# Adding rows on GpSimd ahead of the products with ones, in the second block of a two-block layer

## The reference

```python
def second_block(x, w_in, ...):
    h = rms_norm(x, pre_mix_g)
    a, gate, q, k, v = split(h @ w_in)
    yc = conformer_conv_group(a, gate, ...)       # 1024 channels
    ya = neighbourhood_attention_group(q, k, v, rpb)
    mix = concatenate([yc, ya]) @ w_out
    x = x + rms_norm(mix, post_mix_g)             # the MLP's rows
    h = rms_norm(x, pre_mlp_g)
    f = square(relu(h @ w_up)) @ w_down
    return x + rms_norm(f, post_mlp_g)

def conformer_conv_group(a, gate, ...):
    u = depthwise_conv(a * sigmoid(gate), 31 taps) + b_dw
    return silu(layer_norm(u, ln_g, ln_b))        # over the 1024 channels
```

## Time and profile before

| | us |
|---|---|
| timed runs | 2861.81, 2864.57, 2866.37 |
| median | 2864.57 |
| span of the profiled execution | 2856.0 |
| TensorE busy in it | 2747.0 (96%) |
| VectorE busy in it | 2033.0 (71%) |
| ScalarE busy in it | 1360.4 (48%) |
| GpSimd busy in it | 208.1 (7%) |

### The profile page before, as it was taken

One profiled execution on the slowest core, in us unless ns is written; L12 is line 12 of the kernel. 1 busy time (PEld: TensorE's weight loads), 2 busy tenths in 40 slices (PEclk: granted clock), 3 DMA queues, 4 the chain that ended last, 5 costly groups with the idle time before them and its releaser, 6 DMA issues.

```text
span 2856.0 us, 43985 instructions
## 1 busy us (share of the span) xinstructions
PE 2747.0 (96%) x17404; PEld 2439.8 (85%) x17404; DVE 2033.0 (71%) x2983; ACT 1360.4 (48%) x2169; POOL 208.1 (7%) x180
## 2 busy tenths in 40 slices
PE   6988999999999999999999999999999999999997
PEld 6888778888889888888888889998788888888886
DVE  7898786777797886555556688996567566575665
ACT  3445653343444544444444554465654444444454
POOL 0231000000002000000000080111110000000001
PEclk9999999999999999999999999999999999999999
DMA  9864255656787686555555555554445555555553
GB/s 392 314 228 134 95 172 186 198 192 206 236 304 268 217 305 226 191 188 188 191 185 192 187 169 169 177 165 139 153 130 182 190 187 191 187 190 189 188 190 127
DMA packets 158461, 565.31 MB, mean 198 GB/s; under 512 B 17584, under 2 KB 21936, under 8 KB 158256
## 3 DMA queue, kind: packets, MB, share of 16 engines
q1 hardware_dynamic: 158256, 562.50, 58.9%
HBM read 560.33 MB, written 2.10 MB: 197 GB/s over the span
## 4 chain that ended last, share of the span: by engine, by line
PE 85%; DVE 9%; ACT 3%; issue 2%; DMA 1%; SPq 0%; POOL 0%; DVEq 0%; ACTq 0%; POOLq 0%
PE BK L350 20%; PE BK L348 19%; PE BK L351 10%; PE BK L347 10%; PE BK L353 6%; PE BK L355 5%; PE BK L354 5%; DVE LO L657 2%; PE BK L435 2%; ACT HI L517 1%; DVE ADA L653 1%; DVE B L865 1%; DVE B L707 1%; PE BK L360 1%; PE BK L461 1%
## 5 line engine op out<-in xcount | busy, mean ns | idle before, releaser
L517 ACT ACTIVATE HI<-RAW 128x1024 fp32r<-128x1024 f32 x825 | 875.1, 1061 | 1253.7 <-PE BK L348 862.3
L657 DVE TENSOR_TENSOR LO<-RAW,HI 128x1024 fp32r<-128x1024 f32 x825 | 1017.9, 1234 | 376.2 <-ACT HI L517 373.0
L350 PE MATMUL BK<-H,HI 128*128 128x512 f32 x2528 | 1009.5, 401 | 9.0 <-DVE LO L657 8.5
L348 PE MATMUL BK<-H,HI 128*128 128x512 f32 x2496 | 985.3, 396 | 0.0
L351 PE MATMUL BK<-H,LO 128*128 128x256 f32 x2528 | 703.0, 278 | 0.0
L347 PE MATMUL BK<-H,LO 128*128 128x256 f32 x2496 | 698.2, 280 | 0.4 <-DVE H L703 0.2
L353 PE MATMUL BK<-H,HI 128*128 128x256 f32 x1840 | 545.6, 296 | 33.6 <-DVE B L707 15.7
L347 PEld LDWEIGHTS BK<-H,LO 128*128 128x128 f32 x2496 | 469.7, 188 | 111.8 <-DVE H L703 2.0
L351 PEld LDWEIGHTS BK<-H,LO 128*128 128x128 f32 x2528 | 477.0, 189 | 99.7 <-issue 1.0
L354 PE MATMUL BK<-H,HI 128*128 128x256 f32 x1840 | 523.8, 285 | 0.0
L355 PE MATMUL BK<-H,LO 128*128 128x256 f32 x1840 | 523.6, 285 | 0.0
(11 more groups left out here) (244 smaller groups left out, 1870.5 us busy)
## 6 DMA issues: line engine op xcount, KB each, us to landing
RAW<-wst_dram SPq DMA_DIRECT2D x825, 512.0 KB, 3.9
RAW<-wada_dram SPq DMA_DIRECT2D x155, 512.0 KB, 4.5
EARLY<-wada_dram SPq DMA_DIRECT2D x37, 512.0 KB, 7.8
EARLY<-wst_dram SPq DMA_DIRECT2D x33, 512.0 KB, 6.7
X<-xT_dram SPq DMA_DIRECT2D x8, 512.0 KB, 8.8
B<-bias_dram SPq DMA_DIRECT2D x32, 128.0 KB, 3.4
out_dram<-X SPq DMA_DIRECT2D x3, 512.0 KB, 2.7
CN<-consts_dram SPq DMA_DIRECT2D x1, 840.0 KB, 8.1
```

Of the source, the lines that this page charges most:

```text
L348: e.matmul(bk[:, :], hh, H[:, k, :], start=False, stop=last, skip_group_check=True).then_inc(S["tile"], 1)
L350: e.matmul(bk[:, :], hh, H[:, k, :], start=first, stop=False, skip_group_check=True)
L517: e.activation(HI[:, u % NHL, :], raw_at(slot), ACT.Copy).then_inc(S["hi"], 1)
L657: e.tensor_tensor(LO[:, u % NHL, :], raw_at(slot), HI[:, u % NHL, :].bitcast(f32), sub).then_inc(S["lo"], 1)
```

## The change

GpSimd gets two new steps. `conv_add` adds two rows of 128x256, with its own semaphore `cv_g`. `rows_add` adds a pair of rows (128x512) into another pair. With them:

- The convolution's rows are added into CSUM, row to row, as each pair's taps end, seven additions in all; `conv_sum` is then one product.
- The first centred square goes to CSQ without a buffer of TE, the other seven squares are added to it, and one product (`conv_sum` again) takes the place of eight. It is emitted behind the last addition, at the place where the eighth product stood. A buffer of TE is free again when its addition is done.
- In `mlp_rows` the squares of pairs 2 to 7 and the last are added into rows 0 and 1, seven additions of 128x512, and two products at the end take the place of sixteen.

```diff
--- before.py
+++ after.py
@@ -193,7 +193,7 @@
 
 SIGNALS = ("tile", "hi", "lo", "ada", "mod_p", "mod_v", "pre_a", "pre_v", "ev_a", "ev_v", "ev_g", "ev_p",
            "st_a", "st_v", "st_g", "st_p", "ad_v", "l2_a", "l2_v", "l2_p", "gd_p", "gd_a", "gd_v", "at_p", "at_a",
-           "at_v", "at_g", "cv_a", "cv_v", "cv_p", "spin")
+           "at_v", "at_g", "cv_a", "cv_v", "cv_p", "cv_g", "spin")
 LOADS = tuple(f"raw{i}" for i in range(NRAW + NEARLY)) + tuple(f"bias{i}" for i in range(4)) + ("cols", "consts", "x", "pos", "x2", "out")
 
 
@@ -283,6 +283,7 @@
         CA = [B1[:, 9 + j, :] for j in range(8)]
         BB = [B2[:, 13 + i, :] for i in range(4)]
         MEAN = B2[:, 17, :]
+        CSUM, CSQ = B1[:, 17, :], B1[:, 18, :]
         Y = [B2[:, i, :] for i in range(16)]
         Z = [B1[:, i, :] for i in (8, 9, 10, 11, 16, 17, 18, 19)]
         YA = [B2[:, i, :] for i in range(16)]
@@ -489,21 +490,15 @@
                     r = e.matmul(bk[o:o + 64, 128 * qb:128 * qb + 128], vt[:, c, o:o + 64], t[:, 128 * c:128 * c + 128], start=(c == 0), stop=(c == 1))
                 r.then_inc(S["at_p"], 1)
 
-            def conv_sum(bk, ready, free):
+            def conv_sum(bk, src, ready, free):
                 q.wait_ge(ready, free)
-                for j in range(8):
-                    r = e.matmul(bk[:, 0:256], cn("ones"), CA[j], start=(j == 0), stop=(j == 7))
-                r.then_inc(S["cv_p"], 1)
-
-            def conv_square_sum(bk, j, t, square, free):
-                q.wait_ge(square, free)
-                e.matmul(bk[:, 0:256], cn("ones"), t, start=(j == 0), stop=(j == 7)).then_inc(S["cv_p"], 1)
+                e.matmul(bk[:, 0:256], cn("ones"), src, start=True, stop=True).then_inc(S["cv_p"], 1)
 
             walk(dict(tile=tile, mod_sum=mod_sum, spin=spin, stat_add=stat_add, stat_sum=stat_sum, acc2_sum=acc2_sum, rope_turn=rope_turn, ba_turn=ba_turn,
                       cumulate=cumulate, row_sum=row_sum, spread=spread, g_spread=g_spread, g_heads=g_heads, g_turn=g_turn,
                       g_turn_mt=g_turn_mt, g_pair=g_pair, g_ws=g_ws, g_state=g_state, g_out=g_out, turn=turn,
                       mla_scores=mla_scores, mla_values=mla_values, norm_turn=norm_turn, na_scores=na_scores, na_values=na_values,
-                      conv_sum=conv_sum, conv_square_sum=conv_square_sum))
+                      conv_sum=conv_sum))
 
         def scalar(e):
             q = Engine(e, S)
@@ -914,11 +909,19 @@
                 q.wait_ge(loaded)
                 e.tensor_tensor(BB[i % 4], BB[i % 4], cn("nm"), add).then_inc(S["at_g"], 1)
 
+            def conv_add(dst, a, b, ready, free, before):
+                q.wait_ge(ready, free, before)
+                e.tensor_tensor(dst, a, b, add).then_inc(S["cv_g"], 1)
+
+            def rows_add(dst, src, squares, before):
+                q.wait_ge(squares, before)
+                e.tensor_tensor(dst, dst, src, add).then_inc(S["st_g"], 1)
+
             def part_add(dst, t, copied):
                 q.wait_ge(copied)
                 e.tensor_tensor(dst, dst, t, add).then_inc(S["ev_g"], 1)
 
-            walk(dict(part_add=part_add, square_add=square_add, scaled_square=scaled_square, bias_mask=bias_mask))
+            walk(dict(part_add=part_add, conv_add=conv_add, rows_add=rows_add, square_add=square_add, scaled_square=scaled_square, bias_mask=bias_mask))
 
         def walk(mine, log=None):
             w = Walk(mine)
@@ -2015,25 +2018,36 @@
                         if n % CONV_STEP == 0:
                             yield
                     conv_tok[a:a + 2] = k
+                    if a == 0:
+                        csum = do("conv_add", "cv_g", CSUM, CA[0], CA[1], k, b2_free, None)
+                    else:
+                        csum = do("conv_add", "cv_g", CSUM, CSUM, CA[a], k, None, csum)
+                        csum = do("conv_add", "cv_g", CSUM, CSUM, CA[a + 1], k, None, csum)
                 for _ in xg:
                     yield
-                later(conv_norm(conv_tok[7]), 2)
+                later(conv_norm(csum), 2)
 
             def conv_norm(ready):
                 bi, bk, fr = mbank.get()
-                m = do("conv_sum", "cv_p", bk, ready, fr)
+                m = do("conv_sum", "cv_p", bk, CSUM, ready, fr)
                 yield
                 k = do("conv_mean", "cv_v", bk, m, b2_free)
                 mbank.release(bi, k)
                 yield
-                b2, sq_bk, fr = mbank.get()
+                sq = None
                 for j in range(8):
                     conv_tok[j] = do("conv_center", "cv_v", j, k, m)
+                    if j == 0:
+                        sq = do("conv_square", "cv_a", CSQ, j, conv_tok[j], b2_free)
+                        yield
+                        continue
                     i, t, ft = te.get()
                     a = do("conv_square", "cv_a", t, j, conv_tok[j], ft)
                     yield
-                    m2 = do("conv_square_sum", "cv_p", sq_bk, j, t, a, fr)
-                    te.release(i, m2)
+                    sq = do("conv_add", "cv_g", CSQ, CSQ, t, a, None, sq)
+                    te.release(i, sq)
+                b2, sq_bk, fr = mbank.get()
+                m2 = do("conv_sum", "cv_p", sq_bk, CSQ, sq, fr)
                 yield
                 r = yield from rsqrt_steps(RS[:, 0, :], RS[:, 1, :], sq_bk[:, 0:256], 1.0 / 1024, 1e-5, m2, need(r_tok, "r12"))
                 mbank.release(b2, r)
@@ -2221,33 +2235,26 @@
 
             def mlp_rows():
                 bi, bk, fr = mbank.get()
-                due = []
-
-                def sums():
-                    m = None
-                    for j, k in due:
-                        m = do("stat_add", "st_p", bk, Y[j], j == 0, j == 15, k, fr)
-                    del due[:]
-                    return m
+                sq = [None]
                 for a, b in [(0, 1), (1, 2)] + [(j, j + 2) for j in range(2, 16, 2)]:
                     rb = RS[:, 0, :].unsqueeze(1).broadcast_to([128, b - a, 256])
                     k = do("tensors", "ev_v", rows_of(B2, a, b), rows_of(B2, a, b), rb, mult, [rs_tok] + y_tok[a:b])
                     k = do("tensors", "ev_v", rows_of(X, a, b), rows_of(X, a, b), rows_of(B2, a, b), add, [k] + x_tok[a:b])
-                    sums()
                     for j in range(a, b):
                         x_tok[j] = k
                         s = split(H1, j, X[:, j, :], k, h1_free2, scale=col("pre_mlp", j))
                         next(s)
                         if j == a:
-                            sq = do("square", "st_a", rows_of(B2, a, b), rows_of(X, a, b), k, None)
-                            due += [(i, sq) for i in range(a, b)]
+                            k2 = do("square", "st_a", rows_of(B2, a, b), rows_of(X, a, b), k, None)
+                            sq[0] = do("rows_add", "st_g", rows_of(B2, 0, 2), rows_of(B2, a, b), k2, sq[0]) if a > 1 else k2
                             yield
                         h_tok[j] = whole(s)
                         yield
                 do("root_table", "st_a", n=0)
                 yield
                 yield
-                m = sums()
+                for j in range(2):
+                    m = do("stat_add", "st_p", bk, Y[j], j == 0, j == 1, sq[0], fr)
                 yield
                 r_tok["rx"] = yield from rsqrt_steps(RS[:, 0, :], RS[:, 1, :], bk[:, 0:256], 1.0 / 2048, 1e-6, m, k, loaded=True)
                 mbank.release(bi, r_tok["rx"])
```

## The result

The changed kernel takes 2867.67 us, median of 11 runs (2865.63 to 2875.44); the kernel before, in 11 runs with it, 2861.69. The ratio is 1.0023, interval 1.0014 to 1.0033: +6.0 us, forecast +5.4. That is just over the 0.2% that bound "same", with the bound inside the interval: a little slower.

The account below looks back on a forecast made before the run. VectorE was taken to pace the taps, TensorE the norm, VectorE and ScalarE the MLP's rows. Terms +1.5 - 1.4 + 5.3 = +5.4 us on a median of 2864.57 gave 2870.0 us, range 2861 to 2876.

Parts of the forecast that it names:

- Part 3: MLP's rows: last addition's wait 1.0, holds of VectorE 2.7 and a clock drop 1.6 give +5.3 us, bounds 1.5 and 8.9.
- Price of a product: TensorE's sums: each removed product is worth 0.43 us, from eight products taking 3.45 us on the chain.
- Part 1: Convolution's taps: seven sum additions on GpSimd hold up VectorE, +1.5 us, bounds 0 and 3.8.
- The first addition: Taps stage, first pair of rows: its hold of saturated VectorE comes through whole, 0.58 us.
- the second pair: Taps stage: two additions behind these taps delay VectorE by 0.34 and 0.58, lengthening TensorE's softmax wait by 0.9 us.
- Part 2: Convolution's norm: 6.0 us of products saved, 3.0 lost waiting for GpSimd behind a mask, 1.6 to the clock: -1.4 us.
- The clock's 1.6: Convolution's norm: after TensorE's wait for the squares, four microseconds at a granted clock of 0.61 lose 1.6 us.
- Rival (b): Convolution's norm: the squares' seventh addition isn't behind a waiting mask; total +0.8 us, 2865.4 us; chance 0.18.
- The holds: MLP's rows: GpSimd's additions delay VectorE's H rows by 0.65 to 0.68 us in four pairs, nothing in two; sum 2.7.
- The last addition's wait: End of the MLP's rows: the final product waits for GpSimd's last addition, 1.17 us long, starting 1.04 us later than before.
- Rival (a): MLP's rows: GpSimd's 512-column addition costs 1.46 us, low clock lasts twice as long; total +10.5, 2875 us; chance 0.24.
- Rival (c): All stages: TensorE's path counts everywhere, GpSimd is hidden; 2852.6 us, or -4.5 and 2860.1 in a weaker form; chance 0.08.

Follow-up runs that it names:

- c1: Against the kernel before, only the convolution's row sum moved to GpSimd, additions beside the taps and one product; squares and MLP as before: 2861.72 us, ratio 1.0000.
- m4: MLP's row squares alone on GpSimd, convolution as before, plus seven unused products on TensorE ahead of the two final ones: 2867.94 us, ratio 1.0015 against before.
- m3: MLP's row squares alone on GpSimd with six additions, last pair straight to TensorE, convolution as before: 2865.45 us, ratio 1.0008 against before.
- b1: Against before: convolution's sum added on GpSimd behind the last taps, one product; squares with six additions and two products; MLP as before: 2860.13 us, ratio 0.9994.
- c4: Against before, only the convolution's squares on GpSimd, six additions, eighth square straight to TensorE: 2858.07 us, ratio 0.9985; run again 2859.07 us, 1.0001.
- c2: Against the kernel before, only the convolution's squares on GpSimd with seven additions and one product; sum and MLP as before: 2861.45 us, ratio 0.9997.
- c3: Against before, only the convolution's sum on GpSimd, all seven additions queued behind the last taps, one product: 2861.08 us, ratio 0.9995.

## Why the prediction came out

The total was right, +5.4 for +6.0, and partly by luck. In the two profiles the three parts and what follows the norm come to +9.0: Part 3 was 1.4 higher than forecast, and falls of the clock behind the taps, 2.7, were in no term. That the medians moved by 6.0 and not by 9.0 is because before's profiled execution was 3.7 below its median, a scatter that the sum did not reckon with. The absolute forecast of 2870.0 was 2.3 high, because it started from the median of three runs, 2864.57; over 11 runs it is 2861.69.

**Price of a product.** 0.43 us: right (7 products of the sum -3.03, 14 by the stall -5.98).

**Part 1, +1.5.** Right in size, +1.4 in three of four kernels before the clock falls, but not by its steps. The first addition was put at 0.58 and cost 0.24; the second pair at 0.9 and cost 1.1 to 1.2 (0.7 in c1), for another reason than the one forecast: I had not seen that its additions would queue behind a bias mask and run together with two masks against VectorE. The last two pairs cost nothing, as said. The fall of the clock at the end of that wait (+2.73 in after's profile) was not in the sum; it comes without any addition too (m4 +2.7, m3 and b1 +1.5).

**Part 2.** The mechanism was right, place and releaser: the squares' product waits 2.61 us for 2.97 forecast, behind a mask of 0.72. c4 shows it by its absence. The clock's 1.6 did not come at this stall in after (the products behind it run at 0.28, as before it), and it did in c2 (+1.5 within the stage). A fall of 1.3 came behind the norm in after's profile instead, where others have it too. Rival (b) falls.

**Part 3, +5.3, measured +6.7.** The holds were right: four pairs, 0.70 to 0.72 for 0.65 to 0.68, none in two. The last addition's wait was 1.4 for 1.04: it takes 1.26, not 1.17. By the Trainium skill (GPSIMD Engine Reference, section "Elementwise — side-by-side cycle accounting") the estimate had been 1.28, and the traces agree with it. Rival (a)'s 1.46 falls, and with it a hold of 1.1; its longer low clock came true. For the blocking of VectorE the Trainium skill (SBUF — State Buffer, section "Who interferes with whom") speaks of an exclusive lock, and names the whole instruction where it treats VectorE's two-port modes; in after an H row that starts at 2124.39 and lasts 1.21 was held to 2125.12, 0.19 before the addition's record ends. The term that failed in size is the clock: 1.6 forecast, 2.76 by m4 (one profile), since two falls came in a row, which the upper bound of "twice that" had allowed. The one stand of 9 us came as two, 3.40 and 3.24, because the tiles of rows 8 and 9, which stand ahead of row 10's, waited for the split of their weights, which VectorE ran behind the held H rows; I had left VectorE's splits out there.

**What was missed altogether.** The prediction took falls of the clock as something that a wait makes, at its place. The runs show more: falls come where no wait was added, and the mean clock scatters from run to run by more than the norm's gain of 3 to 5.6 us. Of b1's 5.6 the medians show nothing (+1.4), and its interval allows 4.6 at most. Rival (c), -4.5, is what b1 was built to reach; without the falls its stages reached it, and its time didn't.

## What to carry to other kernels

An addition moved to GpSimd held VectorE for 0.7 us of its 1.27 where both read SBUF, even if nobody waited for the result. Put such additions where VectorE is not the pace, or behind its last instruction, as in c3; that took their cost out of the stage, though no time here shows it. GpSimd works in order: an addition behind a step that waits for a DMA inherits that wait, and giving the last operand straight to TensorE takes it away. And where the granted clock varies from run to run, a gain of 3 us in a stage has to be looked for in the times and mean clocks of many runs, not in one profile.

## What the hardware showed that I had not expected

The granted clock differs between executions of the same code by more than these edits: 0 to 2.99 us behind the norm in kernels with the same code there, 1.47 and 4.53 in two profiles of c4, and a mean of 0.985 to 0.992 over runs of the kernel before. One fall costs up to 1.7 us (10 us at 0.83 from 1712 in before), and two in a row were seen behind the taps (0.66 over 10 us) and in the MLP's rows. GpSimd's 128x512 addition took 1.26 to 1.28 us where VectorE had to wait for it, and 2.2 where it started during a split of VectorE.
